# Three layers in one kernel: x turned as it lands, all decays in the first projection, sine tables between up and down tiles, square sums through PSUM

## The reference

```python
# layer one
h = rms_norm(x, norm_mix_pre); proj = h @ w_in         # q, k, v of attention, and 14 x 128 columns p
attn = sliding_window_sink_attention(q, k, v, rel_bias, sinks)     # 8 heads, window 128, T5 bias
p = p + (p_prev - p) * shift_mix
r, k, v, zw, za, zg = split(p)                                     # RWKV-7, 8 heads of 64
decay = exp(-exp(-softplus(-(w0 + tanh(zw) @ w_decay_up)) - 0.5)); a = sigmoid(a0 + za @ w_iclr_up)
kk = normalized(k * k_k); k = k * (1 + (a - 1) * k_a)
state = state * w_t + sa * (kk_t * a_t) + v_t * k_t                # one step a token
mix = concat(attn, rw) @ w_out; x = x + rms_norm(mix, norm_mix_post)
f = (gelu(conv3(h @ w_up)[gate]) * conv3(h @ w_up)[val]) @ w_down  # h = rms_norm(x, norm_ffn_pre), 4096 wide
x = x + rms_norm(f, norm_ffn_post)
# layers two and three: two kinds of attention each (with partial rotary embedding), then such a feed-forward part
# with silu, 2816 wide; a last rms_norm
```

## Time and profile before

| | us |
|---|---|
| median of 3 runs | 2274.49 |
| lowest, highest | 2271.58, 2274.55 |
| profiled execution, its own time | 2276.84 |
| its span in the profile | 2275.1 |
| PE busy | 2140.0 |
| POOL busy | 987.8 |
| DVE busy | 1224.0 |
| ACT busy | 857.7 |

### The profile page before, as it was taken

How to read it: one execution, slowest core, us unless ns; L and a number is a source line. 1 busy time by engine, 2 the same in 40 slices (tenths; PEclk the granted TensorE clock), 3 DMA queues, 4 the chain that set the end, 5 groups by cost and what they waited for, 6 DMA issues and landing times. The chain is left out here.

```text
span 2275.1 us, 34323 instructions
## 1 busy us (share of the span) xinstructions
PE 2140.0 (94%) x12729; PEld 1721.0 (76%) x12729; DVE 1224.0 (54%) x1927; ACT 857.7 (38%) x1347; POOL 987.8 (43%) x520
## 2 busy tenths in 40 slices
PE   6998896899999999899889999999999889999998
PEld 4666874788888888777667888888677668888887
DVE  3367526777406771422763677721497654777501
ACT  3445224433313332332464333322323744333322
POOL 4224012244544444265553444444365734444442
PEclk8999998899999999899999999999999989999999
DMA  4220012133323333233102333333332003333332
GB/s 127 65 65 26 4 40 70 57 101 100 105 84 91 101 101 102 70 88 83 43 1 75 94 100 101 88 95 104 79 92 74 1 29 93 94 100 92 89 101 87
DMA packets 347082, 177.05 MB, mean 78 GB/s; under 512 B 20835, under 2 KB 344158, under 8 KB 346974
## 3 DMA queue, kind: packets, MB, share of 16 engines
q1 hardware_dynamic: 346476, 175.47, 27.0%
q10 hardware_dynamic: 210, 0.08, 0.0%
q0 software_dynamic: 288, 0.03, 0.0%
HBM read 173.44 MB, written 2.11 MB: 77 GB/s over the span
## 5 line engine op out<-in xcount | busy, mean ns | idle before, releaser
L312 POOL TENSOR_TENSOR wlo<-raw,whi 128x1024 fp32r<-128x1024 f32 (+3 forms) x347 | 792.8, 2287 | 1089.2 <-ACT whi L871 603.9
L325 PE MATMUL banks<-xhi,whi 128*128 128x512 f32 x1688 | 669.1, 396 | 6.7 <-DVE cb L1034 3.9
L326 PE MATMUL banks<-xlo,whi 128*128 128x512 f32 x1688 | 659.1, 390 | 0.0
L327 PE MATMUL banks<-xhi,wlo 128*128 128x512 f32 x1688 | 659.0, 390 | 0.0
L325 PEld LDWEIGHTS banks<-xhi,whi 128*128 128x128 f32 x1688 | 318.0, 188 | 82.6 <-issue 13.6
L326 PEld LDWEIGHTS banks<-xlo,whi 128*128 128x128 f32 x1688 | 318.2, 189 | 68.4 <-issue 3.6
L327 PEld LDWEIGHTS banks<-xhi,wlo 128*128 128x128 f32 x1688 | 318.1, 188 | 67.2
L961 ACT ACTIVATE cb<-banks,conv 128x512 f32<-128x512 f32 x152 | 117.9, 778 | 441.3 <-DVE banks L1023 441.3
L871 ACT ACTIVATE whi<-raw 128x1024 fp32r<-128x1024 f32 (+2 forms) x208 | 204.9, 989 | 181.7 <-DMA raw<-in_ffn_w_out_dram 71.9
L326 PE MATMUL banks<-glo,whi 128*128 128x512 f32 x608 | 236.5, 389 | 0.0
L325 PE MATMUL banks<-ghi,whi 128*128 128x512 f32 x608 | 236.5, 389 | 0.0
(11 more groups left out here) (462 smaller groups left out, 2550.2 us busy)
## 6 DMA issues: line engine op xcount, KB each, us to landing
raw<-in_ffn_w_in_dram SPq DMA_DIRECT2D x88, 512.0 KB, 3.9
raw<-in_w_ffn_up_dram SPq DMA_DIRECT2D x64, 512.0 KB, 4.1
raw<-in_w_ffn_down_dram SPq DMA_DIRECT2D x32, 512.0 KB, 4.0
raw<-in_ev_w_in_dram SPq DMA_DIRECT2D x25, 512.0 KB, 3.9
raw<-in_ffn_w_out_dram SPq DMA_DIRECT2D x32, 384.0 KB, 3.2
raw<-in_ffn_w_out_dram SPq DMA_DIRECT2D x32, 320.0 KB, 2.9
raw<-in_od_w_in_dram SPq DMA_DIRECT2D x20, 512.0 KB, 3.8
raw<-in_w_in_dram SPq DMA_DIRECT2D x16, 512.0 KB, 3.9
```

The lines of the kernel that those rows point to most:

```text
L312: return pool.tensor_tensor(wlo[c][:, 0:n, :], raw[b][:, 0:n, :], whi[c][:, 0:n, :].bitcast(F32), ALU.subtract)
L325: pe.matmul(acc, whi[b][:, k, :], hi(k), start=first and k == 0, stop=False)
L326: pe.matmul(acc, whi[b][:, k, :], lo(k), start=False, stop=False)
L327: mm = pe.matmul(acc, wlo[b][:, k, :], hi(k), start=False, stop=last and k == n - 1)
```

## The change

- Start: ACT's first transfer is the first norm's gain (8 rows of `prow`), which is turned alone; x follows as its halves land, and the bias product and the turn of all 116 rows come after. SP loads weight tile 0 between the halves of x, and `flip` and `sinks` before load 2; the scratch table is written after load 2. POOL splits tiles 0 and 1 before its first add. ACT's squares lag two steps behind `hi`. PE does k-steps 0 to 3 of tile 0, then of tile 1, then both in turn, then tile 2 with the sums inside, the spread, the flips and tile 3.
- Decays: exponentials of all four pairs in the projection at tiles 15, 16, 18, 19, in two pairs of buffers that both stages know (`grow`, `shrink`); the unit keys and their decays one tile later on DVE. In `rwkv` the exponentials go, DVE's four products start without a wait, the bonus jobs lead PE's order, and POOL's low halves of the attention wait for the first `t`.
- `Tables` moves from `project_out` to layer one's first `ffn`, between the up and the down loop, on ACT and on DVE.
- The squares of `project_out` (mixed) go through PSUM banks 4 and 5; `Post` sums its squares in bank 5, and its sums over the partitions stand after k-step 4 of tile 3.

```diff
@@ Post.dve
-                dve.tensor_tensor(acc, self.src[:, 0, :] if k == 1 else acc, self.src[:, k, :], ALU.add).then_inc(self.summed.h, 1)
+                dve.tensor_tensor(acc if k == KD - 1 else bank[5][:, :], self.src[:, 0, :] if k == 1 else bank[5][:, :], self.src[:, k, :], ALU.add)\
+                   .then_inc(self.summed.h, 1)
@@ project_out
+            def square(m):
+                return sq[:, m % 2, :] if mixed is None else bank[4 + m % 2][:, :]
-                    act.activation(sq[:, m % 2, :] if m else acc, to[:, m, :], ACT.Square).then_inc(squared.h, 1)
+                    act.activation(square(m) if m else acc, to[:, m, :], ACT.Square).then_inc(squared.h, 1)
-                        dve.tensor_tensor(acc, acc, sq[:, (m - 1) % 2, :], ALU.add).then_inc(summed.h, 1)
+                        dve.tensor_tensor(acc, square(m - 1), acc, ALU.add).then_inc(summed.h, 1)
@@ ffn
+            tables = Tables(ctx, cosT, sinT) if angles else None
...
-                    up(0, False, tiles_)
-                    lead.pe_sums(pe)
+                    b = (up0 + tiles_) % CUT
+                    pe.wait_ge(w_lo.h, up0 + tiles_ + 1)
+                    for k in range(KD):
+                        pe.matmul(bank[tiles_][:, :], whi[b][:, k, :], hi[:, k, :], start=k == 0, stop=False)
+                        pe.matmul(bank[tiles_][:, :], whi[b][:, k, :], lo[:, k, :], start=False, stop=False)
+                        mm = pe.matmul(bank[tiles_][:, :], wlo[b][:, k, :], hi[:, k, :], start=False, stop=k == KD - 1)
+                        if k == KD // 2:
+                            lead.pe_sums(pe)
+                    mm.then_inc(w_used.h, 1)
@@ ffn, scalar, between the last up turn and the first down tile
+                if tables:
+                    tables.act(act)
@@ ffn, vector, at the same place
+                if tables:
+                    chain = Chain(dve, dve_chain)
+                    tables.dve(dve, chain)
+                    tables.last_dve(dve, chain)
@@ rwkv
-                order += [("turn", 0, 0), ("turn", 1, 0), ("bonus", 0, 0), ("bonus", 1, 0), ("turn", 6, 0), ("turn", 7, 0)]
-                order += [("t", t, 0) for t in range(NT)]
+                order = [("bonus", 0, 0), ("bonus", 1, 0)] + order[:4] + [("turn", 0, 0), ("turn", 1, 0)] + order[4:]
+                order += [("turn", 6, 0), ("turn", 7, 0)] + [("t", t, 0) for t in range(NT)]
-                    pool.wait_ge(expd.h, 4)
-                    pool.tensor_tensor(k[:, 2:4, :], k[:, 2:4, :], em[:, 2:4, :], ALU.mult).then_inc(decayed.h, 1)
-                    pool.tensor_tensor(r[:, 2:4, :], r[:, 2:4, :], ep[:, 2:4, :], ALU.mult).then_inc(decayed.h, 1)
+                    for x, by in ((k, grow), (r, shrink)):
+                        for i in (2, 3):
+                            pool.tensor_tensor(x[:, i, :], x[:, i, :], by[i % 2][:, :], ALU.mult).then_inc(decayed.h, 1)
+                    wait_taken(pool, where["t", 0, 0])
@@ first_stage
-            BONUS, EXPS = (13, 14, 16, 18), 15
+            BONUS, EXPS, UNITE = (13, 14, 16, 18), (15, 16, 18, 19), KSUM + 2
@@ first_stage, pool
+                for m in range(LEAD):
+                    split_lo(pool, s0 + m)
                 for kk in range(1, KD):
                     add(kk)
-                    if kk == 3:
-                        split_lo(pool, s0)
-                    if kk == 5:
-                        split_lo(pool, s0 + 1)
+                    if kk == 4:
+                        split_lo(pool, s0 + LEAD)
@@ first_stage, sync
                 for q in range(2):
                     sp.dma_start(xin[:, :, q * 4 * P:(q + 1) * 4 * P], x[:, :, q * 4 * P:(q + 1) * 4 * P]).then_inc(s_x[q].h, 16)
-                for s in range(RAW):
-                    load(sp, s0 + s)
+                    load(sp, s0 + q)
+                cst_dma(sp, flip[:, :], "flip", s_f)
+                sp.dma_start(sinks[:, :], a["sinks"][0:1, :].broadcast_to([P, NH])).then_inc(s_f.h, 16)
+                load(sp, s0 + RAW)
                 sp.wait_ge(copied.h, 1)
@@ first_stage, tensor
+                pe.wait_ge(s_gain.h, 16)
+                pe.transpose(bank[2][:, 0:KD], prow[0:KD, :], ident[0:KD, 0:KD]).then_inc(gained.h, 1)
...
+                for m in range(LEAD):
+                    pe.wait_ge(w_lo.h, s0 + m + 1)
+                    for k in range(KD // 2):
+                        if m == 0:
+                            pe.wait_ge(ready.h, k + 1)
+                        products(m, k)
+                for k in range(KD // 2, KD):
+                    pe.wait_ge(ready.h, k + 1)
+                    for m in range(LEAD):
+                        mm = products(m, k)
...
+                for k in range(KD):
+                    mm = products(LEAD, k)
+                    if k == KD // 2:
+                        pe.wait_ge(copied.h, 1)
+                        pe.wait_ge(summed.h, KD - 1)
+                        rstd.ready.by(rstd.sums(pe, 0, acc))
@@ first_stage, scalar
+                    if kk in (0, 2, 6):
+                        split_hi(act, s0 + (kk + 1) // 3)
+                    if kk >= 2:
+                        square(kk - 2)
...
-                    i = m - EXPS
-                    if i in (0, 1):
+                    if m in EXPS:
+                        i = EXPS.index(m)
                         act.wait_ge(scanned.h, 4)
-                        act.activation(ep[i][:, :], decay[:, i, :], ACT.Exp, scale=-EHALF).then_inc(expd.h, 1)
-                        act.activation(em[i][:, :], decay[:, i, :], ACT.Exp, scale=EHALF).then_inc(expd.h, 1)
+                        if i >= 2:
+                            act.wait_ge(pooled.h, i - 1)
+                            act.wait_ge(decayed.h, i - 1)
+                        act.activation(shrink[i % 2][:, :], decay[:, i, :], ACT.Exp, scale=-EHALF).then_inc(expd.h, 1)
+                        act.activation(grow[i % 2][:, :], decay[:, i, :], ACT.Exp, scale=EHALF).then_inc(expd.h, 1)
```

More of the change, by code:

```diff
@@ L834, in _, with ffn @@
                             dve.wait_ge(summed.h, m - 2)
-                        dve.tensor_tensor(acc, acc, sq[:, (m - 1) % 2, :], ALU.add).then_inc(summed.h, 1)
+                        dve.tensor_tensor(acc, square(m - 1), acc, ALU.add).then_inc(summed.h, 1)
         state["s"] += n
-    def ffn(w_up, ff, w_down, conv, first, pairs, parts, func, add, acc_to, make_lead=None, tail=None):
+    def ffn(w_up, ff, w_down, conv, first, pairs, parts, func, add, acc_to, make_lead=None, tail=None, angles=False):
         hi, lo, rs, acc = feed["hi"], feed["lo"], feed["rs"], feed["acc"]
@@ L1366, in _ @@
                             wait_taken(pe, n - 4)
+                        if n == where["nt", 0, 0]:
+                            pe.wait_ge(keyed.h, 2)
                         if kind == "p":
@@ L1434, in _ @@
                     pe.wait_ge(lowered.h, 4)
-                    pe.wait_ge(decayed.h, 2)
+                    pe.wait_ge(decayed.h, 4)
                     for ch in range(NCH):
@@ L1681, in first_stage @@
             roots = [roots, mixin]
-            ep, em = (cosT, vT), (sinT, zt)
-            zgated, bonused, expd = sig("zgated"), sig("bonused"), sig("expd")
+            zgated, bonused, expd, pooled, decayed = (sig(x) for x in ("zgated", "bonused", "expd", "pooled", "decayed"))
             s_l, tanhed, ranked, ratesof, scanned, keyed, ksquared, ksummed, bounded, rooted = (
@@ L1686, in first_stage @@
             s_p = sig("s_p", True)
+            s_gain, gained, columned = sig("s_gain"), sig("gained"), sig("columned")
             s_x = [sig("s_x0"), sig("s_x1")]
@@ L1808, in _, with products @@
                     mm.then_inc(turned.h, 1)
-                in_turn(pe, s0, LEAD, hi, lo, ready)
-                pe.wait_ge(copied.h, 1)
-                pe.wait_ge(summed.h, KD - 1)
-                rstd.ready.by(rstd.sums(pe, 0, acc))
+                pe.wait_ge(s_t.h, 48)
+                pe.matmul(bank[3][0:NH, 0:RLEN], table[:, :], hot[:, :], start=True, stop=True).then_inc(rowed.h, 1)
+                pe.wait_ge(s_q.h, 16 * 7)
+                pe.wait_ge(s_p.h, 16 * (len(rows_of) - 8))
+                pe.transpose(bank[2][:, 0:NROW], prow[0:NROW, :], ident[0:NROW, 0:NROW]).then_inc(packed.h, 1)
+                def products(m, k):
+                    b = (s0 + m) % CUT
+                    pe.matmul(bank[m][:, :], whi[b][:, k, :], hi[:, k, :], start=k == 0, stop=False)
+                    pe.matmul(bank[m][:, :], whi[b][:, k, :], lo[:, k, :], start=False, stop=False)
+                    return pe.matmul(bank[m][:, :], wlo[b][:, k, :], hi[:, k, :], start=False, stop=k == KD - 1)
+                for m in range(LEAD):
[8 more added lines that the diff above has]
+                        mm = products(m, k)
+                        if k == KD - 1:
+                            mm.then_inc(w_used.h, 1)
+                pe.wait_ge(w_lo.h, s0 + LEAD + 1)
+                pe.wait_ge(columned.h, 1)
```

(31 more changed lines are left out.)

89 lines of the change are left out of this document (26 added, 63 removed).

## The result

The changed kernel takes 2254.72 us in the median (2251.76 to 2256.37, four runs) against 2273.03 for the kernel before (2269.88 to 2274.55): a ratio of 0.992, 95% interval 0.9903 to 0.9937, or 18.3 us gained (14.3 to 22.0). Run again later, it gave 2254.57 and 0.9923 (0.9909 to 0.9937). Predicted were 2257.0 us and a range of 2248 to 2266.

A forecast was written before the change was run, and what follows sets the result against it. TensorE, busy 94% of the span, was taken as the bound, so only its waits count. Terms 15 + 1 + 2.5 + 6.2 + 0.7 - 7.9 = 17.5 us gave a forecast of 2257.0 us, range 2248 to 2266.

The forecast's parts named there:

- Start: Start of the first projection: x turned earlier, tile 3 starting at 40 us against 55.19; gain 15 us, ends 10 and 17.
- the rule weighed there: Start: POOL's splits block VectorE's two-SBUF-input operations; last low part ready at 27.4, not 25, start ending 0.7 us later.
- the rival of half the gain: Start: ScalarE's wait for tile 1's transfer holds later high parts; tile 3 at 47, 8 us gained, 2264 in all; 17%.
- Decays: Exponentials moved from the recurrence's head into the projection: 1 us at the projection's end, 2.5 at the head; gain 3.5.
- its sign of 22 to 23 us: Recurrence's head: doublings begin 22 to 23 us after the block's start, against 25 before.
- Output projection: End of the output projection: without table arithmetic, and with squares in PSUM, 6.2 us gained, ends 4 and 7.
- Second norm in tile 3: Norm behind the output projection: sums inside tile 3 hide the root's 0.70 us wait; gain 0.7 us, ends 0 and 1.
- Tables at the border: Between up and down loops: sines ahead of ScalarE's splits stall TensorE 5.7 us plus 2.2 cold restart; loss 7.9, ends 3.5 and 11.
- the tables hide: Up/down border: sines do not hold the splits, or the stall is under 2 us; 25 us gained, 2249; chance 10%.
- the down loop that never recovers: First half's down loop never regains its lead after the stall, making the kernel slower: 2278 us; chance 4%.

The follow-up runs named there:

- tables_back: The changed kernel with the sine tables back in the output projection, at tiles 3, 4 and 6: 2254.31 us, ratio 0.9902 to the kernel before.
- squares_in_sbuf: The changed kernel with the squares and their sums back in SBUF, in the output projection and the norm behind it: 2264.2 us in one run.
- sums_after_tile3: The changed kernel with the second norm's sums behind the third up tile again, one execution: 25.28 us from first norm's spread to second's, against 24.60.
- sines_later: The changed kernel with ScalarE's two sines behind its high halves of down tiles 2 and 3: 2248.77 us, ratio 0.989 to the kernel before.
- unit0_first: The changed kernel with ScalarE copying attention unit 0's turned weights and sum out ahead of the exponentials: 2251.23 us, ratio 0.9894 to the kernel before.

## Why the prediction was right, step by step

**Start, +15 against +16.8.** Products from 16.51 (17 predicted), tile 3 at 38.4 (40). The 1.4 us kept for cold products were not needed: with no hole there was no drop. POOL's splits did hold low parts of x, as the earlier trace rows had it (2.27 and 1.76 us for two of them), but these ended ahead of their use, the last low part at 24.9 and not the 27.4 that the rule weighed there gave. What the term lacked is behind tile 3: a wait grown by 1.0 us by a copy held beside POOL, and the drop that mostly follows it. In the medians the start is worth 11 to 13 us. ScalarE's wait for tile 1's transfer held the later high parts as the prediction said (from 15.4 on, said 15), but they still came in time: the rival of half the gain did not come.

**Decays, +3.5 against +5.4.** The projection's end came as said. The mis-sized term is the head: 22.5 us from the block's start were 20.4, so its sign of 22 to 23 us was missed. In the pieces of the working, the "nt" products took 2.0 us where it had 3, and the last "t" with the four turns 5.0 where it left 6.1; the bonus (5.3 against 5.5), two turns (1.9 against 2.2) and the p0 chain (6.2 against 5.7) nearly cancel. It priced the bonus cold, rightly, and the "nt" products as well. But the bonus is what the cold phase falls on. Before, it fell on 256 small products, 6.47 us at clock 0.58 (first row, kernel before), which now take 4.2, while the bonus takes 5.32 us where it took 3.70 warm; but the bonus now runs while VectorE makes the keys, time that TensorE spent idle before:

```profile
206.60:213.20 6.60, 6.47 (x256) 6.33 (x256) 4.94 (x7) 0.70 (x2) 6.39 (x4) 0.58 0.02 5
```

VectorE's masks help too, 0.69 us each with POOL idle, where they had taken 1.34, 1.05, 1.05 and 1.04 (the first of them, kernel before, below). No run parts the order of the bonus, the exponentials and POOL's later low halves from each other.

```profile
211.96 1.34 DVE L1502 TENSOR_TENSOR f<-f,masks 128x512 f32<-128x512 f32 x1
```

**Output projection, +6.2 against +6.3.** The chain of transfer, high half and low half ends it, at 360.83, and TensorE's sums follow at 361.67. The tables were 5.6 of it (tables_back), which leaves 0.7 for the squares; squares_in_sbuf, with the tables away, gives them 1.6. The two do not add, since each is measured with the other change in place. By the Trainium skill ("SBUF — State Buffer", "Who interferes with whom") a VectorE operation with two SBUF inputs contends with a GpSimd one that reads SBUF, and one with at most one SBUF input does not, outside the 2-port modes. The runs agree: the same add took 0.75 us with one input in PSUM and 2.75 with both in SBUF, each beside a split of POOL.

**Second norm in tile 3, +0.7 against +1.3.** 0.7 is the gap (sums_after_tile3), the rest three fewer cold products behind the first norm in that execution (nine against twelve). The prediction saw that adds held by POOL would hold the tile, but it gave the PSUM sums of this norm no price, and its lower end of 0 was too mild. Without them this stage is some 6 us longer, in the one run of squares_in_sbuf.

**Tables at the border, -7.9 against -7.7.** From the first down tile: VectorE free at 6.4 us (6.4 predicted), high halves from 13.0 (13.1), tile 2 at 16.5 (16.5), a wait of 5.45 (5.7), ten products at 1.2 GHz. That the loss was the two sines standing ahead of the two splits is shown by sines_later.

**The sum.** The terms make 17.5 and the profiles 25.2. Of the 7.7 between, 1.8 are the start's, 1.9 the head's, 0.6 the norm's, 0.2 the border's, 0.1 the output projection's, and 3.1 stand in stretches that had no term: 1.9 in the projection, 0.7 in the recurrence, 0.5 behind layer one's first half. These are within the scatter of the same stretches over the other kernels. The medians make 18.3 and 17.2. That they meet the 17.5 so closely is in part luck: the prediction's terms were too small where the changed kernel was early, it had no price for the wait and the drop that being early brought, and these two errors cancel. The mechanism of each term is shown, by the trace or by a run; the start's 15 us as a whole is not divided further than the 4.7 us for the rows. Of the rivals, "the tables hide" was one line of ScalarE's order away; "the start gives half" and the down loop that never recovers did not come. Two sums of the prediction are off in themselves: its numbers for the output projection give 6.3 and not 6.2, and the rival "slower" at its own threshold (seven times 2.6 us) gives 2275 and not 2278.

## What to carry over

Ahead of moving work to where one engine is idle, look at the order of the engine that shares the step: the arithmetic was free on VectorE, and two sines ahead of two splits on ScalarE cost some 7.5 us (7.7 in one pair of profiles, 7.4 in the other), while behind them they cost TensorE nothing. Where a wait is put down to an operation that ended long before, look for the copy that frees the bank. Before anything is made to wait for sums in the middle of a tile, see whether they run beside POOL's splits, and if they do, put them into PSUM.

## What the hardware showed

- One-input operations of VectorE are held by POOL as well: a cast of 128x512 from SBUF to SBUF took 2.50 us beside a split and 0.43 alone, a scale by a column 2.45 against 0.48 (kernel before), the copy of two columns 1.16 against 0.16. The same section of the Trainium skill says that copy, cast and tensor_scalar can enter a 2-port mode and then contend with GpSimd. These rows agree, though the profile does not say in which mode they ran.
- After a stall of 5.45 us ten products ran at 1.2 GHz, and the restart cost 2.1 us (the lead on the kernel before is 26.8 us at the first of them and 24.7 at the second half's first tiles); after 0.9 us (unit0_first, 53.61) none did. After 3.19 us it was none or ten in two executions of one kernel, and 5 to 10 in the others; after 2.16 us for the roots it was nine in the two kernels with unit 0 first, three in tables_back and none in the rest. So executions of this kernel differ by 2 to 4 us in single stages, and a term of that size has to be read from the trace of its stage, not from a median of five.
